# Mixture-of-experts stage: weighing the expert rows as they leave PSUM and adding them up in memory

## What is computed

```python
def routed_experts(t, e_id, w_pair, w1, w3, w2):   # t: 640 x 1024, two experts and two weights per token
    ...
    def blk(args):
        tok_b, w_b, e = args
        xb = t[tok_b]
        hb = jax.nn.silu(xb @ w1[e]) * (xb @ w3[e])
        return (hb @ w2[e]) * w_b[:, None]
    y = lax.map(blk, ...)
    return jnp.zeros_like(t).at[buf_tok].add(y.reshape(-1, t.shape[1]))

def channel_sublayer(x, sh, sc, gt, p):
    h = rms_norm(x, p['g_pre_ffn']) * (1 + sc) + sh
    return x + gt * rms_norm(hierarchical_moe(h, p), p['g_post_ffn'])
```

## Time and profile before

| | |
|---|---|
| median of 3 runs | 1257.73 us (1256.71 to 1259.23) |
| the profiled execution's own time | 1256.07 us |
| its span, first to last instruction | 1254.3 us |
| mean granted TensorE clock | 0.972 |
| busy: TensorE, VectorE, ScalarE, GpSimd | 92%, 67%, 56%, 25% |
| data moved by DMA | 301.27 MB |

### The profile page before, as it was taken

The page is one execution under the profiler, slowest core; times in us unless marked ns, Lnnn a source line. Parts: engine busy times, 40 slices in busy tenths (PEclk is TensorE's granted clock), DMA queues, the critical chain, the costliest instruction groups (busy, mean ns, idle before and its releaser), DMA issues. The chain is left out here.

```text
span 1254.3 us, 16949 instructions
## 1 busy us (share of the span) xinstructions
PE 1156.9 (92%) x5993; PEld 923.7 (74%) x5993; DVE 844.3 (67%) x904; ACT 700.1 (56%) x809; POOL 312.3 (25%) x304
## 2 busy tenths in 40 slices
PE   4889999999788888999769999999999999999996
PEld 2567788777676777888658888888887887888873
DVE  3543132213598763543959999899899988999986
ACT  4222223223566552124537778778877787787764
POOL 4032021000122101000322443344334434433410
PEclk9899999999899997999979999999999999999999
DMA  9633335555500314341379999999999999999964
GB/s 328 231 101 133 127 121 178 176 176 184 204 2 1 119 34 168 119 151 34 118 262 384 372 373 379 377 359 363 361 358 348 362 360 362 359 365 359 362 248 191
DMA packets 151013, 301.27 MB, mean 240 GB/s; under 512 B 12031, under 2 KB 18304, under 8 KB 150322
## 3 DMA queue, kind: packets, MB, share of 16 engines
q1 hardware_dynamic: 135792, 271.07, 60.5%
q0 software_dynamic: 15008, 29.47, 7.0%
q10 hardware_dynamic: 162, 0.05, 0.0%
HBM read 290.68 MB, written 32.67 MB: 258 GB/s over the span
## 5 line engine op out<-in xcount | busy, mean ns | idle before, releaser
L1262 PE MATMUL psum<-w_hi,act_hi 128*128 128x512 f32 (+1 forms) x1288 | 516.9, 401 | 22.5 <-DVE w_lo L1986 6.0
L1264 PE MATMUL psum<-w_hi,act_lo 128*128 128x512 f32 (+1 forms) x1288 | 502.1, 390 | 0.0
L1263 PE MATMUL psum<-w_lo,act_hi 128*128 128x512 f32 (+1 forms) x1288 | 501.1, 389 | 0.0
L1262 PEld LDWEIGHTS psum<-w_hi,act_hi 128*128 128x128 f32 x1288 | 244.3, 190 | 95.7 <-issue 18.1
L1264 PEld LDWEIGHTS psum<-w_hi,act_lo 128*128 128x128 f32 x1288 | 244.2, 190 | 52.0
L1263 PEld LDWEIGHTS psum<-w_lo,act_hi 128*128 128x128 f32 x1288 | 245.0, 190 | 45.5
L1986 DVE TENSOR_TENSOR w_lo<-raw_extra,w_hi 128x2048 fp32r<-128x2048 f32 x96 | 217.3, 2291 | 45.6 <-ACT w_hi L1126 45.6
L1986 DVE TENSOR_TENSOR w_lo<-raw_mix,w_hi 128x2048 fp32r<-128x2048 f32 x96 | 219.3, 2289 | 12.5 <-ACT w_hi L1126 12.5
L1126 ACT ACTIVATE w_hi<-raw_mix 128x2048 fp32r<-128x2048 f32 x96 | 184.0, 1917 | 35.9 <-PE psum L1264 27.3
L1126 ACT ACTIVATE w_hi<-raw_extra 128x2048 fp32r<-128x2048 f32 x96 | 180.6, 1913 | 6.6 <-PE psum L1264 6.6
L1700 DVE TENSOR_TENSOR w_lo<-raw_mix,w_hi 128x2048 fp32r<-128x2048 f32 (+1 forms) x24 | 52.9, 2202 | 164.3 <-ACT w_hi L923 164.3
(11 more groups left out here) (297 smaller groups left out, 1189.5 us busy)
## 6 DMA issues: line engine op xcount, KB each, us to landing
raw_mix<-in_w_e SPq DMA_DIRECT2D x96, 1024.0 KB, 8.1
raw_extra<-in_w_e SPq DMA_DIRECT2D x96, 1024.0 KB, 7.9
raw_mix<-in_w_in SPq DMA_DIRECT2D x16, 1024.0 KB, 6.0
raw_mix<-in_w_ada SPq DMA_DIRECT2D x16, 1024.0 KB, 6.9
ada_first<-in_w_ada SPq DMA_DIRECT2D x8, 1024.0 KB, 19.4
gates_scratch<-rows POOLq DMA_DIRECT2D x20, 256.0 KB, 3.3
y_scratch<-lam SPq DMA_DIRECT2D x1, 5120.0 KB, 16.8
yrow<-gates_scratch POOLq DMA_DIRECT2D x20, 256.0 KB, 4.2
```

Source lines behind the costliest of these rows:

```text
L1262: pe.matmul(out, a_hi(ka_), w_hi[:, kw, :], start=s, stop=False)
L1263: pe.matmul(out, a_hi(ka_), w_lo[:, kw, :], start=False, stop=False)
L1264: ins = pe.matmul(out, a_lo(ka_), w_hi[:, kw, :], start=False, stop=e)
```

## The change

- Every weight is brought to slot order, not only the last expert's: `weigh_pairs` on VectorE makes three bf16 parts of all of them (six instructions, 320 columns), `slot_weights` on TensorE runs 30 matmuls of 32 columns, ScalarE copies the result to `slot_w`, and GpSimd takes an expert's column from it to `w_col` before each scatter.
- The two copies out of PSUM (lines 1201 and 2153) multiply by `w_col`.
- The scatter adds in memory (`compute_op=ALU.add`), so `y_scratch` has one row for each token, 640 in place of 1280. A scatter also waits until the one before has landed. The table of pair rows goes; the gather's table serves both.
- The last expert's weighed rows are split in `y_hi` and `y_lo` (fp32r), and added with a one-hot without weights in four fp32r matmuls for each tile; the identity product of the tile comes first.
- `first_part` and `pair_sum` go. The last tile's final multiply-add and store are done in two halves.

```diff
@@ SyncE
-                    sp.dma_start(raw_pair(i), y_d[2 * P * i:2 * P * (i + 1), :].rearrange("(p k) n -> p (k n)", k=2)).then_inc(x_in[i], 16)
+                    sp.dma_start(raw_pair(i)[:, 0:D], y_d[P * i:P * (i + 1), :]).then_inc(x_in[i], 16)
@@ GpSimd
+            def scatter(n, par, pair, weigh=True):
                 po.wait_ge(moe_sc[par], pair * 16)
+                if weigh:
+                    po.tensor_copy(w_col[:, par:par + 1], slot_w[:, bass.ds(n % NE if isinstance(n, int) else n - NE * rounds[0], 1)]).then_inc(w_col_done, 1)
+                po.tensor_copy(idx_s[:, par:par + 1], tab_g[:, bass.ds(n, 1)]).then_inc(si_done, 1)
                 po.wait_ge(si_done, n + 1)
                 po.wait_ge(moe_ya, n + 1)
                 po.wait_ge(moe_yv, n + 1)
+                po.wait_ge(moe_sc[1 - par], pair * 16 + 16 * par)
                 po.sem_inc(row_dmas, 1)
                 po.indirect_dma_start(out=y_d, out_offset=bass.IndirectOffsetOnAxis(idx_s[:, par:par + 1], 0),
+                                      in_=ysb[:, par * D:(par + 1) * D], in_offset=None, compute_op=ALU.add,
+                                      bounds_check=last_row, oob_is_err=False).then_inc(moe_sc[par], 16)
...
+                po.wait_ge(slot_w_done, 2 + r)
@@ ScalarE
-                ac.activation(ysb[:, par * D:par * D + 512], bank(5), ACT.Copy).then_inc(moe_ya, 1)
+                ac.wait_ge(w_col_done, n + 2)
+                ac.activation(ysb[:, par * D:par * D + 512], bank(5), ACT.Copy, scale=w_col[:, par:par + 1]).then_inc(moe_ya, 1)
+            def last_high(s6):
+                for x in range(2):
+                    ac.wait_ge(moe_mm, s6 + 5 + x)
+                    ac.activation(y_hi[:, x * 512:x * 512 + 512], bank(5 + x), ACT.Copy, scale=slot_w[:, NE - 1:NE]).then_inc(y_hi_done, 1)
...
                 ac.wait_ge(moe_mm, UPR * r + 2)
+                ac.wait_ge(slot_w_mm, 2 + r)
+                ac.activation(slot_w[:, :], bank(7)[:, P:P + NE], ACT.Copy).then_inc(slot_w_done, 1)
@@ TensorE
+            def slot_weights(r):
+                if r == 0:
+                    pe.wait_ge(parts_done, 2)
+                parts = weight_parts[:, :].rearrange("p (n x e) -> p n x e", n=3, x=2 * NT)
+                for x in range(2 * NT):
+                    for n in range(3):
+                        ins = pe.matmul(bank(7)[:, P:P + NE], roc[:, x * P:(x + 1) * P], parts[:, n, x, :], start=(x + n == 0), stop=(x == 2 * NT - 1 and n == 2))
+                ins.then_inc(slot_w_mm, 1)
...
                 up(NS + UPR * r + 1, 2, 2, 0, 0)
                 up(NS + UPR * r + 2, 0, 2, 0, 1)
+                slot_weights(r)
                 with pe.Fori(0, NE // 2 - 1) as i:
...
             for i in range(NT):
+                pe.wait_ge(x_in[i], 32)
...
                 for x in range(2):
-                    pe.matmul(bank(SUM_BANK[i] + x), loh[:, i * P:(i + 1) * P], ysb[:, D + x * 512:D + x * 512 + 512], start=True, stop=False)
-                pe.wait_ge(c_sum, i + 1)
+                    pe.matmul(bank(SUM_BANK[i] + x), ident[:, :], raw_pair(i)[:, x * 512:x * 512 + 512], start=True, stop=False)
                 for x in range(2):
-                    ins = pe.matmul(bank(SUM_BANK[i] + x), ident[:, :], raw_pair(i)[:, x * 512:x * 512 + 512], start=False, stop=True)
+                    if i == 0:
+                        pe.wait_ge(y_lo_done, x + 1)
+                    pe.matmul(bank(SUM_BANK[i] + x), loh[:, i * P:(i + 1) * P], y_hi[:, x * 512:x * 512 + 512], start=False, stop=False)
+                    ins = pe.matmul(bank(SUM_BANK[i] + x), loh[:, i * P:(i + 1) * P], y_lo[:, x * 512:x * 512 + 512], start=False, stop=True)
@@ VectorE
+            def weigh_pairs():
+                parts = weight_parts[:, :].rearrange("p (n x) -> p n x", n=3)
+                weights = rtw[:, :]
+                link(ve.tensor_tensor(weights.rearrange("p (x e) -> p x e", e=NE), ohw[:, :].rearrange("p (x e) -> p x e", e=NE), wk[:, :].unsqueeze(2).broadcast_to([P, 2 * NT, NE]), ALU.mult))
+                for n in range(2):
+                    link(ve.tensor_copy(parts[:, n, :], weights))
+                    link(ve.tensor_tensor(weights, weights, parts[:, n, :], ALU.subtract))
+                ve.tensor_copy(parts[:, 2, :], weights).then_inc(parts_done, 1)
...
+                if last and r == 0:
+                    for x in range(2):
+                        cols = slice(x * 512, x * 512 + 512)
+                        ve.wait_ge(y_hi_done, x + 1)
+                        ve.scalar_tensor_tensor(y_lo[:, cols], bank(5 + x), slot_w[:, NE - 1:NE], y_hi[:, cols].bitcast(F32), ALU.mult, ALU.subtract).then_inc(y_lo_done, 1)
+                    return
...
-                ve.tensor_copy(ysb[:, par * D + 512:(par + 1) * D], bank(6)).then_inc(moe_yv, 1)
+                ve.wait_ge(w_col_done, n + 2)
+                ve.tensor_scalar(ysb[:, par * D + 512:(par + 1) * D], bank(6), w_col[:, par:par + 1], None, ALU.mult).then_inc(moe_yv, 1)
...
                 moe_lo(NS + UPR * r + 4, 3, 2)
+                if r == 0:
+                    weigh_pairs()
```

## The result

The changed kernel takes **1271.97 us** (median of 4 runs, 1268.25 to 1274.17) against 1258.14 us before (4 runs, 1256.71 to 1259.23): 1.0108 times the time before, 95% interval 1.0088 to 1.0127. A second measurement, on another chip, gave 1271.57 us (6 runs) and 1.0111 (1.0092 to 1.0130). The forecast was 1259.7 us, at most 1264.5: wrong by 12 us. The profiled execution took 1270.46 us, its span is 1268.7 us.

The account below looks back on a forecast made before the run. TensorE was taken to bound the loop, VectorE the tail, serial waits the entry. Loop +2.3, entry +5.2, tail -5.5 make +2.0 on the profiled 1256.07 us, 1258.1; that run being 1.7 below the median, 1259.7, range 1255.5 to 1264.5.

Parts of the forecast that it names:

- Loop: the weights applied at the emptying: Expert loop: scalar operands on the emptyings of PSUM banks 5 and 6 lengthen TensorE's chain, +2.3 us, between 0 and 4.5.
- rival (a): Loop: the adding scatter delays the gather behind it on GpSimd's queue, much slower, up to 142 us; chance 10%.
- if it doubled the 6.3: Loop: if adding doubled a scatter's 6.3 us landing and the gather waited for all of it, 142 us.
- The operands: Loop: a per-partition scalar adds 0.09 us to ScalarE's emptying and 0.06 to VectorE's, +2.3 us in all.
- The slack in the expert that loads no table: Loop: some 0.09 us before TensorE's start, taken off 0.15, leaving 0.06 us, 15 times, 0.9 us.
- The small new waits of TensorE on that expert: Loop sign: small new TensorE waits on w_lo in the expert of each pass that does not reload Silu's table.
- The entry: Loop entry: TensorE and ScalarE wait for the slot weights' parts and products, +5.2 us, range 4.6 to 6.2.
- The casts: Entry: three VectorE casts to bf16, between 0.18 and 0.49 us each, taken as 0.40.
- 1.1 us of lost clock: Entry: slow transposes and first matmuls after TensorE's wait lose some 1.1 us, mostly absorbed by an existing 0.89 us wait.
- The tail: After the last product: VectorE bound, -4.6 us to the last multiply-add; with the store -5.5, range -4.5 to -6.6.
- the middle between 0 and 1.9: Tail: the halved last store gains between 0 and 1.9 us, taken as 0.9.
- TensorE's wait on w_lo at 0.45 us: Loop sign: TensorE's wait on VectorE's w_lo split grows to about 0.45 us in place of 0.36.

Follow-up runs that it names:

- e1: The changed kernel with its scatters writing instead of adding, waits and all else kept: 1262.40 us, 1.0040 of the kernel before.
- e2: The kernel before with its scatters adding to memory rows that hold zeros instead of writing them: 1269.91 us, 1.0102.
- e3: The kernel before with a scalar operand of 1.0 on both instructions that empty PSUM: 1261.77 us, 1.0037.
- e16: The changed kernel with an expert's rows in a third layout, 16 consecutive slots on 16 engines by the skill's map: 1262.35 us, 1.0037.
- e5: The kernel before with each expert's rows written twice by plain scatters, the copy to memory nobody reads: 1271.77 us, 1.0115.
- e11: The kernel before with the scalar operand of 1.0 on ScalarE's half of the emptying alone: 1260.33 us, 1.0026.
- e7: The changed kernel with a quarter of one of six weight loads left out for each expert but the first: 1261.72 us, 1.0032.
- e9: The changed kernel unaltered, measured again on one chip beside e10: 1271.57 us, 1.0111 of the kernel before.
- e12: The changed kernel with an expert's first 16 rows laid out 8 partitions apart: 1266.25 us, 1.0066.
- e10: The same kernel as e4, measured again on one chip beside e9: 1262.85 us, 1.0048.
- e4: The changed kernel with the table of slot weights made earlier, its products right behind the first expert's transposes: 1262.69 us, 1.0034.

## Why the prediction was wrong

**The step that failed is "Loop: the weights applied at the emptying"**, +2.3 us where 12.4 were measured. It priced two instructions of the change in the loop and not the third. The adding scatter stands in the prediction once, as rival (a), and there only as latency: what it delays behind it on GpSimd's queue. Its other price, time of the DMA engines that the weight loads share, was in no term. The runs showed in its place that the adding scatter costs the loop 8.3 to 9.7 us (e1, e2), because weight loads land in 12.7 us in place of 8 and ScalarE waits for them, and that the operands cost 3.3 us (e3). The row that should have stopped me was to be had before: in the loop the queues fill 97.1 + 4.6% of the DMA engines, and that no engine waits for a load there does not say how much longer a load may take. What ran out was not the sum (e16 spends as much and waits for no load) but, as far as chains and layouts can tell, the few engines that serve partitions 0, 1, 2 and on, where a scatter of 14 rows already runs in chains of four. The bound for an operation without a row ("if it doubled the 6.3") was put on its landing time, which rose by 1.3 us only and harmed nobody. The gather landed in 8.0 us, so rival (a) did not come about as told; a small form of it stands in e5 alone, 3.2 us.

**The operands** themselves: +3.3 us (e3), inside the 0 to 4.5, above the 2.3. ScalarE's emptying took 0.69 us and VectorE's 0.74, the +0.09 and +0.06 of the earlier trace rows; e11 gives ScalarE's alone 2.7 us, 30 times 0.09. The slack in the expert that loads no table, which I took off, is not there: in e3 that expert grew from 17.79 to 17.93 us, by both instructions, where the sum had 0.06, and the one that loads it from 18.41 to 18.49, near its 0.09. The small new waits of TensorE on that expert, which the text named as a sign, did not come: e1 has 14 waits as before.

**The entry**: right in its mechanism and place. The casts took 0.33 us, between the bounds; the parts were ready at 654.5, on a start 1.5 us later than before (forecast 653.3), the wait 4.2 us (4.4). Against 31.02 us the entry took 5.2 to 5.3 us more in five traces (e1, e7, e9, e12, e16), which is the forecast, and 6.3 in the first, a little over the range of 4.6 to 6.2, whose last interval was 20.20 us against 19.00 in e9. The traces show why: from 654 to 664 us the mean granted clock is 0.67 in the first and 0.83 in e9, and the products behind the transposes run at half speed until 660.5 us in the first and until 657.4 in e9. So the lower level lasted longer in the first trace, which the text's 1.1 us of lost clock did not hold.

**The tail**: -4.9 and -0.9 us against -4.6 and -0.9; 17.3 us where the text said 17.5. Over all traces the piece after the last multiply-add is 5.3 us in the mean with the whole last store (seven kernels) and 4.7 us with the halved one (twelve), so the store gave 0.6, and the 0.9 between the two first traces was in part luck. 0.6 is the estimate that the prediction drew from the Trainium skill (DMA: Bandwidth & Descriptors, Anatomy of one DMA); the middle between 0 and 1.9 was the worse choice.

**The signs to look for** were the right ones for entry and tail. For the loop the text named TensorE's wait on w_lo at 0.45 us. It was 0.49 in a quiet expert (1034.97), but the longest had grown to 1.6, with a load behind it, and no sign was named for that.

## What to carry to other kernels

Price each DMA that a change touches twice: by its latency for those that wait for it, and by the time it takes on the DMA engines for those that share them. If it moves only some partitions of a tile, ask also how its rows spread over the engines: here the loads beside it landed in 12.7, 8.9 or 8.0 us by the layout alone. Laying the rows out so that, by that map, each 16 successive ones lie on 16 engines cost two instructions on GpSimd and gave back all that the adding scatter had taken.

## What the runs showed of the hardware

- A scatter that adds takes 327 ns for a row of 4096 bytes on its DMA engine, one that writes 159 ns, and GpSimd's issue of it 1.60 us in place of 1.02 to 1.03.
- Rows from neighbouring partitions follow one another, four in a chain, 0.40 us a link when they are added: the scatter of 12 rows, from partitions 0 to 11, ran as three chains of four. With nearly the same engine time (6.8, 6.9 and 7.1%), the layout alone moved the landing of 1 MB loads from 12.7 us (rows in partitions 0, 1, 2 and on) over 8.9 (8 apart) to 8.0 (the third layout), and the loop from 571 over 567 to 563 us.
- A busy share of the DMA engines near 100% did not tell a loop that is bound by loads (after) from one that is not (before). The consumers' waits and the landing times did.
- An operand of one value per partition costs 0.09 us on ScalarE's emptying of 128x512 from PSUM and 0.06 us on VectorE's.
- Behind the same stop of TensorE the granted clock differs from one execution to the next: the last expert took 32.9, 34.4 or 35.7 us at a mean granted clock of 1.00, 0.95 or 0.90 (e10, after, e4).
